# Order within the slots of a three-engine software pipeline: where reciprocal, scaling, evacuation and rounding stand in VectorE's and ScalarE's queues

## The reference

```python
sc = jnp.einsum('bkgqd,bksd->bkgqs', qg, k).astype(jnp.float32) * scale
o = jnp.einsum('bkgqs,bksd->bkgqd', jax.nn.softmax(sc, axis=-1).astype(v.dtype), v)
mix = jnp.einsum('bse,ed->bsd', mix, w_o[l])
```

## Time and profile before

| | us |
|---|---|
| median of three runs | 1906.06 (1905.43 to 1907.14) |
| the profiled execution, its own time | 1905.94 |
| its span in the trace | 1904.2 |
| TensorE matmuls busy | 1839.6 |
| VectorE busy | 1348.1 |
| ScalarE busy | 1004.2 |
| mean granted TensorE clock | 0.993 of full speed |

### The profile page before, as it was taken

The page is one execution under the profiler, slowest core; times in us unless marked ns, Lnnn a source line. Parts: engine busy times, 40 slices in busy tenths (PEclk is TensorE's granted clock), DMA queues, the critical chain, the costliest instruction groups (busy, mean ns, idle before and its releaser), DMA issues.

```text
span 1904.2 us, 33674 instructions
## 1 busy us (share of the span) xinstructions
PE 1839.6 (97%) x13104; PEld 1662.2 (87%) x13104; DVE 1348.1 (71%) x2158; ACT 1004.2 (53%) x1614; POOL 78.5 (4%) x98
## 2 busy tenths in 40 slices
PE   8999999999999998999999999999999999989998
PEld 8868999986899986899989789998979998869997
DVE  6758888775888876887877588886555556766555
ACT  7775334767533477533364453346864335764333
POOL 3003000000000000000000000003400000000000
PEclk9999999999999998999999999999999999999999
DMA  8538988533788842688853278885335554325552
GB/s 308 183 118 251 350 314 308 189 133 119 286 324 308 307 167 70 254 328 311 324 216 134 91 299 331 306 309 212 141 136 199 180 195 166 121 101 200 185 190 88
DMA packets 62058, 416.57 MB, mean 219 GB/s; under 512 B 9008, under 2 KB 9200, under 8 KB 13312
## 3 DMA queue, kind: packets, MB, share of 16 engines
q1 hardware_dynamic: 56016, 401.33, 57.0%
q0 software_dynamic: 5936, 13.79, 2.5%
HBM read 413.90 MB, written 3.19 MB: 219 GB/s over the span
## 4 chain that ended last, share of the span: by engine, by line
PE 83%; DVE 7%; ACT 7%; issue 2%; DVEq 1%; ACTq 1%; DMA 0%; SPq 0%
PE psu L533 35%; PE psy L701 18%; PE psy L595 6%; PE psy L587 5%; PE psu L550 4%; PE psy L641 4%; PE psy L574 2%; ACT work L839 2%; PE psu L781 2%; DVE wlo L951 1%; ACT work L851 1%; PE psy L664 1%; DVE x L1221 1%; PE pso L767 1%; PE psm L801 1%
## 5 line engine op out<-in xcount | busy, mean ns | idle before, releaser
L942 ACT CAST whi<-raw 128x2048 fp32r<-128x2048 f32 (+1 forms) x281 | 536.2, 1908 | 598.9 <-PE psu L533 398.7
L951 DVE TENSOR_TENSOR wlo<-raw,whi 128x2048 fp32r<-128x2048 f32 (+5 forms) x306 | 646.8, 2115 | 270.0 <-ACT whi L942 269.1
L533 PE MATMUL psu<-hlo,whi 128*128 128x256 f32 x1920 | 536.0, 279 | 0.0
L533 PE MATMUL psu<-hhi,wlo 128*128 128x256 f32 x1920 | 535.9, 279 | 0.0
L533 PE MATMUL psu<-hhi,whi 128*128 128x256 f32 x1920 | 535.9, 279 | 0.0
L533 PEld LDWEIGHTS psu<-hhi,whi 128*128 128x128 f32 x1920 | 360.9, 188 | 2.3
L533 PEld LDWEIGHTS psu<-hlo,whi 128*128 128x128 f32 x1920 | 360.9, 188 | 2.3
L533 PEld LDWEIGHTS psu<-hhi,wlo 128*128 128x128 f32 x1920 | 361.0, 188 | 0.0
L1153 DVE CUSTOM_DVE_ANT_0 ada_raw<-ada_raw,cvec 128x1024 f32<-128x1024 f32 x192 | 227.0, 1220 | 2.8 <-DMA ada_raw<-ada 2.8
L701 PE MATMUL psy<-whi,ahi 128*128 128x512 f32 x528 | 210.2, 398 | 0.0
L701 PE MATMUL psy<-wlo,ahi 128*128 128x512 f32 x528 | 207.9, 394 | 0.0
(11 more groups left out here) (342 smaller groups left out, 2893.5 us busy)
## 6 DMA issues: line engine op xcount, KB each, us to landing
raw<-wts SPq DMA_DIRECT2D x280, 1024.0 KB, 4.8
ada_raw<-ada SPq DMA_DIRECT2D x96, 1024.0 KB, 4.9
gain<-gate_rows POOLq DMA_DIRECT2D x8, 512.0 KB, 4.0
dense_bias<-rel_bias POOLq DMA_DIRECT2D x32, 64.0 KB, 10.3
nab<-dense_bias SPq DMA_DIRECT2D x2, 1024.0 KB, 7.6
ada_raw<-fox_rows POOLq DMA_DIRECT2D x4, 512.0 KB, 12.3
cb<-cst POOLq DMA_DIRECT2D x1, 1408.0 KB, 9.4
cb<-cst SPq DMA_DIRECT2D x1, 1056.0 KB, 10.1
```

The lines of the kernel that those rows point to most:

```text
L533: last = mm(psu[:, bank, cc * SEQ:(cc + 1) * SEQ], a[:, cols], h[:, kt, :], start=(kt == 0 and j == 0), stop=(kt == KT - 1 and j == 2))
L942: nc.scalar.copy(whi[:, part_of(c), 0:n], raw[:, slot_of(c), 0:n]).then_inc(hi_done, 1)
L951: last = nc.vector.tensor_tensor(wlo[:, part_of(c), cols], raw[:, slot_of(c), cols], whi[:, part_of(c), cols].bitcast(f32), ALU.subtract)
```

## The change

The reciprocal goes behind the maximum (and behind the evacuation) in VectorE's slot, the scaling behind the exponential and the rounding in ScalarE's. The evacuation of a pair of items goes to the start of VectorE's next slot, except for the last item. The roundings go to the slot after the one that `turn` names, on both engines, except number 7. The slots of TensorE do not change: `pe_mix1_turn` goes on reading `turn`, and so do the slabs. The argument `divide_first`, with which two slots of SWA had the evacuation first, goes away.

```diff
+    def rounds(self, h):
+        return [m for at, m in self.turn.items() if at == (h if m == 7 else h - 1)]
...
-        def dve_steps(dve, I0, items, plan, h, g, divide_first=False):
-            dve_roots(dve, I0, items, plan, h)
-            k = plan.value(h)
-            if k is not None and divide_first:
+        def dve_steps(dve, I0, items, plan, h, g):
+            k = plan.value(h - 1)
+            if k is not None and items[k]["pair"] is None and k < len(items) - 1:
                 dve_divide(dve, I0, items, plan, k)
             k = plan.score(h)
             second = None
...
             k = plan.value(h)
-            if k is not None and not divide_first:
+            if k is not None and (items[k]["pair"] is not None or k == len(items) - 1):
                 dve_divide(dve, I0, items, plan, k)
             if second is not None:
                 dve_negated(dve, I0, items[second], second, score_at(plan, second))
-            if h in plan.turn:
-                m = plan.turn[h]
+            dve_roots(dve, I0, items, plan, h)
+            for m in plan.rounds(h):
                 dve_turn(dve, m, g, psu[:, 1, 0:SEQ] if plan is MIX and m < 2 else columns(plan, m))
```

In ScalarE's three mixers (`act_mix1`, `act_swa`, `act_fox`) alike:

```diff
                 act_copy(act, I0, items, MIX, h)
-                act_normal(act, I0, items, MIX, h)
                 act_exp(act, I0, items, MIX, h)
...
-                if h in MIX.turn:
-                    m = MIX.turn[h]
+                for m in MIX.rounds(h):
...
+                act_normal(act, I0, items, MIX, h)
```

More of the change, by code:

```diff
@@ L1810, in act_swa @@
                 act_copy(act, I0, items, SWA, h)
-                act_normal(act, I0, items, SWA, h)
                 if SWA_HEADS.get(h + 1, 0) == 4:
@@ L1818, in act_swa @@
                     turned(SWA_HEADS[h])
-                if h in SWA.turn:
-                    m = SWA.turn[h]
+                for m in SWA.rounds(h):
                     act_turn(act, DEPTH1, c0 + 6, m, g, columns(SWA, m), o_evac, I0 + 2 * m + 2)
+                act_normal(act, I0, items, SWA, h)
                 if h == 23:
@@ L1833, in act_fox @@
                 act_copy(act, I0, items, FOX, h)
-                act_normal(act, I0, items, FOX, h)
                 act_exp(act, I0, items, FOX, h)
@@ L1846, in act_fox @@
                         nc.scalar.copy(dst, fold(src, NT, 256)).then_inc(bank_free, 1)
-                if h in FOX.turn:
-                    m = FOX.turn[h]
+                for m in FOX.rounds(h):
                     act_turn(act, DEPTH1, c0 + 13, m, g, columns(FOX, m), o_evac, I0 + 2 * m + 2)
+                act_normal(act, I0, items, FOX, h)
                 if h == 28:
@@ L1954, in dve_swa @@
             for h in range(SWA.slots):
-                dve_steps(dve, I0, items, SWA, h, g, divide_first=SWA_ROPE.get(h - 1, 0) >= 3)
+                dve_steps(dve, I0, items, SWA, h, g)
                 if h in SWA_ROPE:
```

## The result

The changed kernel takes 1918.91 us (median of four runs, 1918.42 to 1920.42), the kernel before beside it 1905.74 (1904.84 to 1907.14): ratio 1.007, interval 1.0052 to 1.0087. It is slower by 13.2 us, where +9.2 (1915.0) was forecast. The profiled execution took 1920.42 us, its span is 1918.6.

The account below looks back on a forecast made before the run. TensorE was taken as the bound, busy 97% of the span, its waits being what an order can win. Mixed stages +19.4, windowed -10.2, forgetting and evacuation 0 gave +9.2 us, 1915.0; range 1904 to 1924, the forecast's own 1909 to 1922.

Parts of the forecast that it names:

- The waits of the mixed stage: TensorE waits for late roundings 0 to 3 in each mixed attention stage: 4.4, 2.8, 1.65 and 3.0 us.
- S(12,13): Scores of items 12 and 13 in the mixed stage; TensorE's wait for them was to become 0.45 us.
- row block 0: Output block in the mixed stage; TensorE's wait for it was to become 0.9 us.
- the slow clock: Mixed stages: TensorE at about half clock after waits, two 3.4 us stretches for one, +1.7 us each, bounds -1.7 and +5.1.
- The windowed stages: Two windowed attention stages of the first block: 3.5 and 6.7 us shorter, together -10.2, bounds -4 and -22.
- the ring: Reciprocal, scaling, next exponential, rounding, next reciprocal between ScalarE and VectorE; cutting it was to save a 0.81 us scaling per slot.
- the modulation's products: Two VectorE products of 1.14 us each, first windowed stage, slot 18; still ahead of a maximum, leaving a 2.5 us wait.
- The forgetting stage: Forgetting attention stage, 1.4 us idle: late rounding was to change it by 0, between -1 and +1 us.
- The evacuation: A pair's copy one slot later, covered by that slot's weight quarter and transposes: 0 us.
- A: Rival, chance 0.14: faster, 1889.5 us; late rounding hidden, mixed stages at 0, windowed ones win their 16.4 us idle time.
- B: Rival, chance 0.16: no change, 1906.1 us; slow clock falls into waits, +5.2 per mixed stage, -10.2 for the windowed.
- C: Rival, chance 0.10: slower still, 1922 us; one score bank keeps 1.8 + 1.75 us of waits in both mixed stages, +7.1.

Follow-up runs that it names:

- filled: The changed kernel with matmuls of zeros into free banks ahead of the four rounding waits of each mixed stage; 1907.45 us, ratio 1.0001.
- mix_rounds_back: The changed kernel with roundings 0 to 4 of the mixed stages back in their old slots; 1890.98 us, ratio 0.9927.
- best_b: `best_a` with the modulation's products one slot later in the windowed stage; 1887.14 us, ratio 0.9898.
- best_a: `mix_rounds_back` with the pairs' evacuation also back in its own slot; 1891.55 us, ratio 0.9923.
- ring_only: The kernel before with only the reciprocal moved behind the maxima and the scaling behind the exponential and rounding; 1896.75 us, ratio 0.9953.
- round_late_only: The kernel before with only the roundings one slot later, number 7 staying; 1927.41 us, ratio 1.0117.
- evac_back: The changed kernel with the pair's evacuation back in its own slot; 1919.18 us, ratio 1.0071.
- late01: The changed kernel with roundings 2, 3 and 4 of the mixed stages back, 0 and 1 staying late; 1906.15 us in one run.
- late23: The changed kernel with roundings 0, 1 and 4 of the mixed stages back, 2 and 3 staying late; 1903.18 us in one run.

## Why the prediction was right, and where its sizes were off

**The sign and the mechanism held.** The forecast, slower through waits behind the late roundings, is what happened. The time, 1918.91, lies within the forecast's own range (1909 to 1922), 3.9 us above the 1915.0.

**The waits of the mixed stage** were forecast at 4.4, 2.8, 1.65 and 3.0 us; the trace has 4.26, 2.71, 1.67 and 2.59. The two that were to shrink came out at 0.2 for S(12,13) (0.45) and 0.8 for row block 0 (0.9). Sum 12.5, forecast 13.2. The times inside the first held as well: weight rounding at 96.11 (95.87), `alo` 0 at 103.24 (103.0), TensorE on at 103.81 (103.6). The walk along ScalarE's queue was enough for the first. The second, 2.71 against 2.8, is luck in part: rounding 1 came 4.7 us after the start of S(14) and not 3.9, and S itself covered 2.0 and not 1.06, both because of the slow clock, and the two errors cancel. At full clock, in `filled`, it is 3.8, close to the forecast.

**The slow clock is the term that was mis-sized.** I took two stretches of 3.4 us where one was, +1.7 us, with +5.1 as the bound. The same matmuls ran 4.8 us longer, and with the longer chain it is 5.7 to 7.2 us (`filled`). There are 16.7 us in the first mixed stage, most of it in one piece. Three sums that start from `mix_rounds_back` separate the parts: back to before it is 2.2 and 2.7 us (what the rest of the change wins), up to `filled` 7.4 and 7.9 (the waits), and from there to the changed kernel 6.7 and 7.2 (the clock). -2.2 + 7.4 + 6.7 = +11.9, and -2.7 + 7.9 + 7.2 = +12.4, against 9.7 forecast. That the second stage has the same loss as the first, as assumed, is right within 0.5 us.

**The windowed stages** gave 4.6 and 6.5 us, forecast 3.5 and 6.7. A clock of 0.98 over 80.1 us is 3.2 us slow in the first, half of what I took. So of its 4.6 us only 1.3 are idle time (7.1 to 5.8) and 3.3 are matmuls at a faster clock; I had forecast 1.7 and 1.8. TensorE's waits there (700 to 790) are those forecast:

```profile
PE pso L772 <- ACT work L830: 2.6, 3, 1.6
PE psu L786 <- DVE nmax L906: 2.5, 1, 2.5
PE psy L646 <- ACT work L1801: 0.8, 1, 0.8
...
```

The sum was right and its attribution was not. I wrote that the late rounding costs or wins nothing there; alone it wins 3.8 and 4.2 us, and the ring alone 3.3 and 2.4. My walk through the timeline had both in place at once, so it could not see which did it. And I named the modulation's products as what keeps the 2.5 us wait; `best_b` shows it: one slot later the wait is 0.2, and the stage 2.4 us shorter than in `best_a` (286.14 against 288.56, from the same rows of its chain).

**The forgetting stage** was taken as 0 between -1 and +1 and lost 1.1. A wait of 0.7 us for the copy of the transposes (L830) is new in it. `ring_only` has no such wait and +0.2 there, `round_late_only` 0.3 us of it and +0.5, and `evac_back` all 0.7: it comes with the late rounding, in full only with both halves, and not with the evacuation. **The evacuation** at 0: `evac_back` agrees.

**The rivals.** A, all hidden, failed at the point named for it: rounding 1 was to be done within 1.06 us of the start of S(14); S starts at 107.89 and TensorE goes on at 112.60, 4.7 later. `mix_rounds_back`, where rounding 1 is in its old slot, comes near the time of A (1890.98 against 1889.5), but by other parts: the mixed stages win 2.2 and 2.7 us there, the windowed ones 4.6 and 6.5 and not 16.4. B, no change because the slow clock falls into waits: the stretch grew instead, and `filled` is what B would have been, a kernel with the waits and without their clock, at 1907.45 against B's 1906.1. C, the one score bank: the waits for the exponential fell from 3.9 to 0.2 us with the same banks, so an order was enough. The Trainium skill (Perfetto Trace Analysis, Optimization Strategy) says that a bubble that repeats can mean too little room in SBUF or PSUM; here it was an in-order queue, and the measurement decides. By weight-load busy time, which the Trainium skill (Perfetto Trace Analysis, Identifying the Most-Contended Engine) names as a measure of headroom, 21 us were open in a mixed stage, an estimate from the earlier trace rows. The best order found wins 2.1 and 2.8 us in the two of them; no run here shows more, which does not prove that there is none.

## What to carry to other kernels

Before an instruction is put later in an in-order queue, look up for each instance when its reader wants it: the same move by one slot won 4 us in stages whose readers came slots later, and lost 14 where the reader stood in the next slot. Two moves that cut a ring between engines are one edit; price them together and then one at a time, because either alone can do nothing or harm. And price a wait of TensorE of some microseconds twice, once as idle time and once as the work done at half clock behind it: here 7.4 us of waits brought 6.7 us more in the traced executions.

## What the hardware showed that was not expected

In these traces shorter waits cost little clock and longer ones much. Before, waits of 1.8 us and, 1.1 us after its end, 0.8 were followed by one stretch of 3.4 us at 0.55. In the changed kernel, with a wait of 4.26 us and one of 2.71 that begins 6.1 us after its end, the clock was at 0.50 for 13.6 us in a row. Behind its wait of 1.67 it stayed at 1.00 (127 to 130), and behind that of 2.59 it was 0.63 from 133 to 136 and 0.85 from 136 to 140, some 3.4 us slow. `late01`, with the two long waits, and `late23`, with the other two, have 125.3 and 121.9 us of matmuls in stretches of the first mixed stage (13 to 147 and 13 to 142.3) in which `mix_rounds_back` has 121.1 (13 to 138): most of the price of the clock goes with the first two waits. No run varies the length of one wait, so where it turns is not shown.

With matmuls of zeros in the place of the waits the clock stayed at 1.00 for the whole stage. So this time can be won back without a faster chain: `filled` is 11.5 us faster than the changed kernel while TensorE does 42 matmuls more in each mixed stage. What would come of fillers in `best_b`, where the mixers' waits left are 1.6 us or less, was not tried.
